# Recurrence of a gated DeltaNet layer: regrouped instruction orders, and the second decay matrix made by transposes of the first

## The reference, cut to what matters

```python
gcum = jnp.cumsum(gc, axis=-1)
decay = jnp.exp(jnp.where(causal, gcum[..., :, None] - gcum[..., None, :], -jnp.inf))
a_mat = jnp.where(strict, jnp.einsum('bhncd,bhnsd->bhncs', kb, kc) * decay, 0.0) + jnp.eye(c)
sol = lax.linalg.triangular_solve(a_mat, rhs, left_side=True, lower=True, unit_diagonal=True)
qk = jnp.einsum('bhncd,bhnsd->bhncs', qc, kc) * decay
```

## Time and profile before

| | us |
|---|---|
| Median of 3 runs (lowest, highest) | 969.88 (968.77, 970.65) |
| The profiled execution, its device time | 969.67 |
| Its span | 967.9 |
| TensorE busy in the span | 926.8 |
| VectorE busy | 583.4 |
| ScalarE busy | 520.0 |

### The profile page before, as it was taken

How to read it: one execution, slowest core, us unless ns; L and a number is a source line. 1 busy time by engine, 2 the same in 40 slices (tenths; PEclk the granted TensorE clock), 3 DMA queues, 4 the chain that set the end, 5 groups by cost and what they waited for, 6 DMA issues and landing times.

```text
span 967.9 us, 14303 instructions
## 1 busy us (share of the span) xinstructions
PE 926.8 (96%) x5437; PEld 781.8 (81%) x5437; DVE 583.4 (60%) x967; ACT 520.0 (54%) x920; POOL 24.2 (2%) x47
## 2 busy tenths in 40 slices
PE   6999999999999999999999999998889999999998
PEld 6988978797888877888878788997567788888776
DVE  5767875666566564555544665656857555554465
ACT  6644545766767456444434548245865644444352
POOL 5100000000000000000000000000000000000000
PEclk9999999999999999999999999999999999999999
DMA  9941202021112556767545654420024566555552
GB/s 318 333 138 44 88 0 88 12 77 44 45 45 92 206 163 212 239 219 249 197 161 186 205 174 159 147 88 2 1 88 143 168 193 191 175 191 176 170 187 101
DMA packets 105899, 138.30 MB, mean 143 GB/s; under 512 B 4585, under 2 KB 76786, under 8 KB 105842
## 3 DMA queue, kind: packets, MB, share of 16 engines
q1 hardware_dynamic: 103650, 130.15, 42.1%
q0 software_dynamic: 2160, 7.36, 2.2%
q10 hardware_dynamic: 32, 0.01, 0.0%
HBM read 136.45 MB, written 1.05 MB: 142 GB/s over the span
## 4 chain that ended last, share of the span: by engine, by line
PE 79%; ACT 10%; DVE 8%; issue 2%; DMA 0%; ACTq 0%; SPq 0%; DVEq 0%
PE ps L497 16%; PE ps L499 16%; PE ps L498 16%; PE ps L476 4%; PE ps L481 4%; ACT w_hi L1105 4%; PE ps L483 4%; PE ps L482 4%; DVE w_lo L1565 4%; PE ps L712 3%; PE ps L730 3%; PE ps L945 1%; PE ps L991 1%; ACT qkvT L1499 1%; PE ps L615 1%
## 5 line engine op out<-in xcount | busy, mean ns | idle before, releaser
L1565 DVE TENSOR_TENSOR w_lo<-w_raw,w_hi 128x2048 fp32r<-128x2048 f32 (+2 forms) x100 | 220.7, 2207 | 210.3 <-ACT w_hi L1105 210.1
L1105 ACT ACTIVATE w_hi<-w_raw 128x2048 fp32r<-128x2048 f32 (+2 forms) x100 | 184.4, 1844 | 191.6 <-PE ps L499 149.4
L497 PE MATMUL ps<-w_hi,x_hi 128*128 128x512 f32 x480 | 193.1, 402 | 7.3 <-DVE gdn L1776 2.2
L499 PE MATMUL ps<-w_hi,x_lo 128*128 128x512 f32 x480 | 187.6, 391 | 0.0
L498 PE MATMUL ps<-w_lo,x_hi 128*128 128x512 f32 x480 | 187.3, 390 | 0.0
L497 PEld LDWEIGHTS ps<-w_hi,x_hi 128*128 128x128 f32 x480 | 90.2, 188 | 29.8 <-issue 7.4
L499 PEld LDWEIGHTS ps<-w_hi,x_lo 128*128 128x128 f32 x480 | 90.1, 188 | 19.4
L498 PEld LDWEIGHTS ps<-w_lo,x_hi 128*128 128x128 f32 x480 | 90.3, 188 | 16.7
L481 PE MATMUL ps<-x_hi,w_hi 128*128 128x256 f32 x320 | 91.9, 287 | 0.3 <-DVE w_lo L1611 0.3
L497 PE MATMUL ps<-w_hi,big 128*128 128x512 f32 x224 | 89.9, 401 | 1.0 <-DVE w_lo L1565 1.0
L482 PE MATMUL ps<-x_lo,w_hi 128*128 128x256 f32 x320 | 90.7, 283 | 0.0
(11 more groups left out here) (309 smaller groups left out, 1513.9 us busy)
## 6 DMA issues: line engine op xcount, KB each, us to landing
w_raw<-in_ffn_w_in SPq DMA_DIRECT2D x88, 512.0 KB, 4.6
w_raw<-in_ffn_w_out SPq DMA_DIRECT2D x40, 512.0 KB, 4.0
w_raw<-in_gdn_w_in SPq DMA_DIRECT2D x28, 512.0 KB, 4.7
gdn<-in_gdn_w_in SPq DMA_DIRECT2D x20, 512.0 KB, 8.7
w_raw<-in_gdn_w_out SPq DMA_DIRECT2D x16, 512.0 KB, 4.5
w_raw<-in_ple_w_gate SPq DMA_DIRECT2D x16, 512.0 KB, 4.6
w_raw<-in_kv_w SPq DMA_DIRECT2D x12, 512.0 KB, 4.2
qkvT<-in_cmp_w POOLq DMA_DIRECT2D x8, 512.0 KB, 5.5
```

What stands on the lines that cost most here:

```text
L497: mm(o, hi, w_h, start=first and kk == 0, stop=False, skip_group_check=True)
L499: return mm(o, lo, w_h, start=False, stop=end and kk == n - 1, skip_group_check=True)
L1105: A(whi[:, place(stage, q), c0:c0 + n], ring_raw(u) if stage == "qkv" else raw[:, q, 0:n], ACT.Copy).then_inc(S["hi_done"], 1)
L1565: V.tensor_tensor(wlo[:, s, c0:c0 + n], ring_raw(u) if stage == "qkv" else raw[:, q, 0:n], whi[:, s, c0:c0 + n], ALU.subtract).then_inc(S[ ...
```

## The change

- `dQ` is no longer made by products and an exponential. `decay_rows` now begins with the bf16 mask product, and `decay_cols` is four transposes of each chunk's `dA`, which ScalarE copies to `dQ`.
- The opening runs `decay_cols(0)`, `keys(0)`, `keys(1)`, `decay_cols(1)`. `decay_cols` waits for `dA`'s exponential, and `keys_decayed` waits for the transposes, since it overwrites `dA`.
- `gate_columns` is cut in two: `decay_columns` (13 operations) runs at loop index 12, `beta_columns` (6) after the loop; `triangles(0, ...)` runs ahead of `conv(14)`. ScalarE's three exponentials run at loop index 11, with a return to the SiLU table.
- VectorE's copy of the sums goes ahead of the split at index 10.
- `silu_qkv` 13, 14, 15 are spread over j = 0, 1, 2. `o_squares(1, j)` moves behind the copies of `dQ` of j+1.
- The first z part waits for one chunk of the scaled values at a time.
- `split("gout", 1)` goes ahead of `o_out(1, 3)`; `split("kv", 1, 2)` goes into the middle of `block_copies`.

```diff
-            pe.wait_ge(S["ba_dve"], N_BA)
+            pe.wait_ge(S["ba_dve"], N_DECAY)
...
+                o = bank((0, 4)[c], 4, P)
+                mm(o, identb[:, :], over(causb[:, :], 1, 4), start=True, stop=False, skip_group_check=True)
                 for n in range(4):
-                    last = mm(bank((0, 4)[c], 4, P)[:, n, :], gtri[:, c, n, :], tri_gt[:, :], start=True, stop=True)
+                    last = mm(o[:, n, :], gtri[:, c, n, :], tri_gt[:, :], start=False, stop=n == 3, skip_group_check=True)
...
-                    if j < 2 and c == 0:
-                        pe.wait_ge(S["silu_done"], 10 if j == 0 else 16)
+                    if c == 0:
+                        pe.wait_ge(S["silu_done"], (10, 13, 14, 16)[j])
...
-                    o = bank((5, 1)[c], 4, P)
-                    mm(o, causb[:, :], over(identb[:, :], 1, 4), start=True, stop=False, skip_group_check=True)
-                    mm(o, tri_gt[:, :], gtri[:, c], start=False, stop=True, skip_group_check=True).then_inc(S["dQ_ps"], 1)
+                    pe.wait_ge(S["dA_ex"], 2 * j + c + 1)
+                    for n in range(4):
+                        last = transpose(bank((5, 1)[c], 4, P)[:, n, :], dA[:, c, n, :])
+                    last.then_inc(S["dQ_ps"], 1)
...
-                    if part == 0:
-                        pe.wait_ge(S["bv_sb"], 2 * j + 2)
                     for a in range(TT):
+                        if part == 0:
+                            pe.wait_ge(S["bv_sb"], 2 * j + 1 + a)
...
+                decay_cols(0)
                 keys(0)
-                decay_cols(0)
+                keys(1)
                 decay_cols(1)
-                keys(1)
...
+                if u == 11:
+                    act.wait_ge(S["ba_dve"], 4)
+                    A(sm[2], sm[2], ACT.Exp, scale=-1.0).then_inc(S["ba_act"], 1)
+                    A(alog[:, :], alog[:, :], ACT.Exp).then_inc(S["ba_act"], 1)
+                    A(sm[6], balog[:, :, 0:HV], ACT.Exp, scale=-1.0).then_inc(S["ba_act"], 1)
+                    table(ACT.Silu)
             act.wait_ge(S["l2_dve"], 3)
             A(kr, kk, ACT.Sqrt).then_inc(S["l2_root"], 1)
-            act.wait_ge(S["ba_dve"], 4)
-            A(sm[2], sm[2], ACT.Exp, scale=-1.0).then_inc(S["ba_act"], 1)
-            A(alog[:, :], alog[:, :], ACT.Exp).then_inc(S["ba_act"], 1)
-            A(sm[6], balog[:, :, 0:HV], ACT.Exp, scale=-1.0).then_inc(S["ba_act"], 1)
+            table(ACT.Exp)
...
-                    A(dQ[:, c], bank((5, 1)[c], 4, P), ACT.Exp).then_inc(S["dQ_ex"], 1)
+                    A(dQ[:, c], bank((5, 1)[c], 4, P), ACT.Copy).then_inc(S["dQ_ex"], 1)
+                if j:
+                    o_squares(1, j - 1)
...
-                if j == 0:
-                    for u in (13, 14, 15):
-                        silu_qkv(u)
+                if j < 3:
+                    silu_qkv(13 + j)
...
                 o_squares(0, j)
+                if j == 3:
+                    split("gout", 1)
                 if j < 3:
                     decay_a(j + 1, 1)
                 o_out(1, j)
-                o_squares(1, j)
+                if j == 3:
+                    o_squares(1, j)
...
-            block_copies(A, 0, S["ablk_act"])
-            split("kv", 1, 2)
+            block_copies(A, 0, S["ablk_act"], lambda: split("kv", 1, 2))
...
             for u in range(15):
+                if u == 10:
+                    dve.wait_ge(S["sum_ps"], 1)
+                    V.tensor_copy(tkr[0:16, :], ps[0:16, 0, 0:T]).then_inc(S["sum_sb"], 1)
+                if u == 12:
+                    decay_columns()
                 if u < 14:
                     split("qkv", u % 2, (u + 2) // 2)
                 if u == 14:
-                    gate_columns()
+                    dve.wait_ge(S["cst_pool"], N_CST)
+                    triangles(0, 0)
+                    triangles(0, 1)
                 conv(u)
...
+            beta_columns()
             conv(15)
...
                     dve.wait_ge(S["kq_ps"], 2 * j + c + 1)
-                    dve.wait_ge(S["dA_ex"], 2 * j + c + 1)
+                    dve.wait_ge(S["dQ_ps"], 2 * j + c + 1)
```

More of the change, by code:

```diff
@@ L22 @@
 N_BA = 23
+N_DECAY = 17
 N_CST = 22
@@ L246, in build, with block_copies @@
             S[name] = sem(name)
-        def block_copies(copy, v, done):
+        def block_copies(copy, v, done, between=None):
             for par in range(2):
+                if par and between:
+                    between()
                 for e in range(2):
@@ L1352, in _ @@
                 delta(j)
-            split("gout", 1)
             act.wait_ge(S["on_dve"], 4)
@@ L1665, in head_columns, with decay_columns @@
                 V.tensor_scalar(kk, hcol[:, :, HK:], EPS, None, ALU.add).then_inc(S["l2_dve"], 1)
-            def gate_columns():
+            def decay_columns():
                 dve.wait_ge(S["ba_act"], 3)
-                dve.wait_ge(S["l2_root"], 1)
                 ba(V.tensor_scalar(sm[3], sm[2], 2.0, None, ALU.add))
-                ba(V.tensor_scalar(sm[6], sm[6], 1.0, None, ALU.add))
-                ba(V.reciprocal(kr, kr))
-                ba(V.reciprocal(krr, kk))
                 done()
                 ba(V.reciprocal(sm[3], sm[3]))
-                ba(V.reciprocal(beta, sm[6]))
                 done()
                 ba(V.tensor_tensor(sm[3], sm[2], sm[3], ALU.mult))
-                b3 = beta.rearrange("p a (h r) -> p a h r", r=2)
-                ba(V.tensor_tensor(acol.rearrange("p a (h r) -> p a h r", r=2), b3, over(krr, 3, 2), ALU.mult))
-                ba(V.tensor_tensor(bcol.rearrange("p a (h r) -> p a h r", r=2), b3, over(kr, 3, 2), ALU.mult))
                 done()
@@ L1695, in gate_columns, with beta_columns @@
                 ba(stt(out=gdec, in0=sm[1], scalar=-1.0, in1=over(alog[:, :], 1, TT), op0=ALU.mult, op1=ALU.mult))
+                assert n_ba[0] == N_DECAY, n_ba[0]
+                done()
+            def beta_columns():
+                dve.wait_ge(S["l2_root"], 1)
+                ba(V.tensor_scalar(sm[6], sm[6], 1.0, None, ALU.add))
+                ba(V.reciprocal(kr, kr))
+                ba(V.reciprocal(krr, kk))
+                done()
+                ba(V.reciprocal(beta, sm[6]))
+                done()
+                b3 = beta.rearrange("p a (h r) -> p a h r", r=2)
+                ba(V.tensor_tensor(acol.rearrange("p a (h r) -> p a h r", r=2), b3, over(krr, 3, 2), ALU.mult))
+                ba(V.tensor_tensor(bcol.rearrange("p a (h r) -> p a h r", r=2), b3, over(kr, 3, 2), ALU.mult))
                 assert n_ba[0] == N_BA, n_ba[0]
@@ L1717, in _ @@
                     decay_inputs()
-                if u == 10:
-                    dve.wait_ge(S["sum_ps"], 1)
-                    V.tensor_copy(tkr[0:16, :], ps[0:16, 0, 0:T]).then_inc(S["sum_sb"], 1)
                 if u == 12:
                     head_columns()
-            dve.wait_ge(S["cst_pool"], N_CST)
-            triangles(0, 0)
-            triangles(0, 1)
+            beta_columns()
             conv(15)
```

## The result

The changed kernel takes **959.08 us** (median of 6 runs, 957.75 to 960.95) beside 969.41 us (median of 6 runs, 968.74 to 970.65) for the kernel before: a ratio of 0.9894 with a 95% interval of 0.9881 to 0.9907, 10.3 us less. A second series gave 958.52 beside 969.46 us, 0.9882 (0.9866 to 0.9899). The forecast was 957.7 us, a gain of 12.0 us; 10.3 us came, 1.7 less. The profiled execution has a span of 956.8 us and a device time of 958.89 us; the earlier trace rows belong to a span of 967.9.

What follows compares the result with a forecast made beforehand. TensorE, busy 926.8 of 967.9 us, was taken as the bound; -1.4 + 0.3 - 3.7 - 2.9 - 2.2 - 0.7 - 1.4 = -12.0 us against 969.67 gave 957.7 us, range 955.8 to 961.8.

Steps and rivals of the forecast that it cites:

- Parts 1 and 2: Sums copied earlier, removing the wait behind unit 11, -1.4 us; decay columns inside the projection, unit 14 0.3 us late.
- Part 3: First opening: triangles and decay sums ready earlier, 1.6 us wait and low clock go; -3.7 us, bounds 2.0 and 4.1.
- Part 4: Later openings, j = 1 to 3: 4.2 us gained, 1.3 back in closing parts; net -2.9 us, bounds 1.1 and 3.4.
- Part 5: First z part: chunk 0 products run while VectorE scales chunk 1, four waits go; -2.2 us, bounds 0 and 2.8.
- (b): Levels: VectorE's z quarter and update pace level 1, no z-part gain, openings lose another 1 us; 960.9 us, chance 0.12.
- Part 6: `gout` high part moved ahead of `o_out(1, 3)`, -0.7 us; `kv` split started after eight copies, -1.4 us.
- (a): Openings: a turn waits for ScalarE's late exponential in place of the removed product, 1.8 us back; 959.5 us, chance 0.12.
- (c): Start: the clock falls all the same, from the 0.3 us stall and new small waits; 959.4 us, chance 0.08.
- (d): Openings: transposes do not keep the clock up, all four run at 1.2 GHz; slower, 983.7 us, chance 0.03.
- (e): ScalarE's added table switches ahead of unit 14 cost more than the trace row shows; 959.1 us, chance 0.05.
- (f): Openings: a turned tile costs as much as the product it replaces, 5.1 us missing; 962.8 us, chance 0.04.

## Why the prediction was right, and where it was not

**Parts 1 and 2** came out as summed: -1.4 and +0.4 for -1.4 and +0.3. Addition of VectorE's and ScalarE's queues gave the start of the split of unit 14 as 104.6, and it was 104.86. TensorE began unit 14 0.33 us late by the starts of its matmuls, of which the list of waits shows 0.2.

**Part 3** came to -4.0 for -3.7 in the profiled pair, but one term rests on less than the text said. The orders and the wait give 12.38 - 9.99 = 2.4 us with the clock full in both. That is the wait of 1.6 us and the 0.84 us of work that came back with the product, so the 0.4 us charged for new waits did not come. The other 1.6 us are the clock, priced rightly from the windows (1.7) and wrongly tied to the gap: "it fell only behind a gap of 1.6 us" is what one profile showed, and the kernel before keeps its clock in some executions. By the mean clock it lost it in nine of twelve, so the median should still hold most of that term; that the term came in the profiled pair was in part luck.

**Part 4**: -4.3 and +1.3 for -4.2 and +1.3. An opening took 7.46 us where 7.4 was computed, with VectorE arriving just behind TensorE, twice by some 0.2 us where 0.3 us in one place was charged. The closing parts gave back the mask products.

**Part 5 is the step that failed**: "The four waits of 0.54 us go: -2.2 us". Only that of j = 0 went for good. In j = 1 to 3 a table load on ScalarE, 1.28 us with nothing idle around it, stands ahead of a copy that TensorE needs a little later. TensorE's wait for VectorE had brought it there late enough not to notice; with that wait gone, TensorE waited 0.6 us for the load (-1.1 in place of -2.2). I had named VectorE as what would be late next and did not look at ScalarE's timeline in level 1, where the load stood. Of the rivals, **(b)** comes nearest: time given back in the levels, but by another engine and a third of its price. Moving the load shows that without it part 5 is worth 2.9 us, a little over its upper bound of 2.8. So the size was off twice: each stop cost 0.73 us where 0.54 was taken from the list of waits, and three of the four came back for the most part.

**Part 6**: -0.95 for -0.7 and -1.5 for -1.4.

**The other rivals.** (a) is absent: no turn waits for the exponential in TensorE's list. (c): in the profiled execution the clock was 1.00 from 119 to 129, also with the small stops; one of the ten executions has a mean clock of 0.998, and where it fell is not on record. (d): twelve or twenty transposes in an opening, 7.11 of 7.60 us busy at 1.00. The Trainium skill (TensorE: Matmul & The Clock Gate, Part 4: PE-mode transpose) says that a transpose does not count as busy the way a product does; in this mix of transposes and products the trace shows nothing of it. (e): both added loads took 1.28 us with the next instruction 0.01 us behind, so the drain that the Trainium skill states (ScalarE: Activation LUTs, What ACT_TABLE_LOAD costs) did not appear. (f): with the product back the stages are 2.7 us longer, so the turned tile does take work away.

The sum of the misses: part 5 +1.1, the others together -0.7, and +0.5 outside the change (start-up 0.3, the rest behind the recurrence) make the span's -11.1 for -12.0. The medians differ by 10.3. The remaining 0.8 is of the size by which start-up and gate landing move single executions, and was not traced further.

## What to carry to other kernels

When a wait is taken off the bounding engine, read every other engine's timeline in that same stretch: a long instruction with no idle time around it (here a 1.28 us table load) may be covered only because that wait makes the bounding engine come later, and belongs where its own engine stands idle. Two edits that each shorten one stage add up only until the engine behind them becomes the chain (4.0 us separately, 3.0 together). A clock that fell behind a gap in one profile is no rule; profile the unchanged kernel twice more before a term rests on it.

## What the runs showed of the hardware

- The granted clock behind one and the same 1.6 us gap fell to 0.50 in two profiled executions of one kernel and stayed at 1.00 in a third, at a price of 1.6 us; behind gaps of 0.9 and 2.1 us in two variants it stayed at 1.00 in the one execution profiled of each.
- An fp32 transpose of 128x128 costs 0.11 us back to back (eight in 0.87, four in 0.44), one of the two records of 0.11 us into which an fp32 product of 128 columns falls. That made the turned tile cheaper than the product it replaces by 0.63 us for each chunk.
- A switch of ScalarE's table cost 1.28 us and 0.01 to 0.02 us to the next activation, in `98.46 + 1.28` to 99.75 and `220.49 + 1.28` to 221.78, and in the earlier trace rows.
